# A two-layer hybrid step: weight slots of the head, the prompt's queries, and the order of the latent norm

## The reference, cut to what matters

```python
sh1, sc1, g1, sh2, sc2, g2 = split(silu(c) @ w_mod + b_mod, 6)     # modulation
h = rmsnorm(x, norm1) * (1 + sc1) + sh1
z = h @ w_in                                                        # 1024 x 2464
#   conv(768) | q latent 256, kv latent 128, rope 32 | retention q k v g 1024 | pooling 256
ckv = rmsnorm(z_kv, mla_kv_norm); q = rmsnorm(z_q, mla_q_norm) @ w_uq    # latent attention
x = x + g1 * (concat(y_conv, y_mla, y_ret, y_pool) @ w_out)
h = rmsnorm(x, norm2) * (1 + sc2) + sh2
q = h @ w_q                                     # PEER: 8 heads, 128 columns each
s = q . subkeys                                 # two halves x 128 keys a head
eidx, gates = top 16 of the 16 x 16 best pairs, softmax
a = h . u_tab[eidx]; y = sum_k gates * gelu(a) * v_tab[eidx]       # 128 rows of u and v a token
x = x + g2 * y
```

## Time and profile before

| | |
|---|---|
| median of three runs | 2587.06 us (2586.25 to 2589.85) |
| profiled execution | 2589.36 us, span 2587.6 us |
| TensorE matmul busy | 1896.0 us, 73% |
| VectorE busy | 1691.5 us, 65% |
| ScalarE busy | 550.9 us, 21% |
| GpSimd busy | 1518.4 us, 59% |
| moved | 939.90 MB, 363 GB/s over the span |
| mean granted TensorE clock | 0.89 of full |

### The profile page before, as it was taken

The page is one execution under the profiler, slowest core; times in us unless marked ns, Lnnn a source line. Parts: engine busy times, 40 slices in busy tenths (PEclk is TensorE's granted clock), DMA queues, the critical chain, the costliest instruction groups (busy, mean ns, idle before and its releaser), DMA issues.

```text
span 2587.6 us, 19654 instructions
## 1 busy us (share of the span) xinstructions
PE 1896.0 (73%) x5402; PEld 858.3 (33%) x5402; DVE 1691.5 (65%) x3756; ACT 550.9 (21%) x1378; POOL 1518.4 (59%) x1562
## 2 busy tenths in 40 slices
PE   5778985786777555697767677677777777777776
PEld 2354443353232212243342233334422322222222
DVE  0327875777799655566779666677868887554454
ACT  1332223221121101212222122222211121111111
POOL 2004554656677534656656655556667777677774
PEclk8988987898999866897889988788989999999999
DMA  8756996999999999999999999789999999999998
GB/s 291 259 193 248 405 354 238 385 364 399 385 403 409 403 396 371 356 355 405 337 404 383 361 375 383 288 291 385 358 375 409 409 409 409 371 411 409 409 409 323
DMA packets 295971, 939.90 MB, mean 363 GB/s; under 512 B 30692, under 2 KB 44360, under 8 KB 295864
## 3 DMA queue, kind: packets, MB, share of 16 engines
q0 software_dynamic: 222496, 809.28, 80.7%
q1 hardware_dynamic: 71304, 127.38, 13.6%
q10 hardware_dynamic: 2064, 2.00, 0.2%
HBM read 936.55 MB, written 2.00 MB: 363 GB/s over the span
## 4 chain that ended last, share of the span: by engine, by line
DMA 28%; DVE 25%; PE 24%; POOL 10%; issue 7%; ACT 5%; SPq 1%; DVEq 0%; ACTq 0%; POOLq 0%
DMA vbuf<-in_peer_v_dram,eidx 12%; DVE ubuf L2081 11%; DMA ubuf<-in_peer_u_dram,eidx 9%; PE ysum L1190 8%; PE bank L922 5%; POOL vbuf L2138 5%; POOL ubuf L2138 5%; DMA wring<-in_w_mod_dram 4%; DMA wring<-in_w_in_dram 3%; DVE acc L2074 3%; PE bank L1156 2%; PE bank L1141 2%; SPq L819 1%; PE bank L865 1%; DVE scratch L1955 1%
## 5 line engine op out<-in xcount | busy, mean ns | idle before, releaser
L1190 PE MATMUL ysum<-vbuf,diag 128*128 128x512 f32 x2356 | 1205.7, 647 | 356.4 <-DMA vbuf<-in_peer_v_dram,eidx 238.5
L2081 DVE CUSTOM_DVE_ANT_0 ubuf<-ubuf,h_bank 128x1024 f32<-128x1024 f32 x768 | 910.2, 1219 | 383.1 <-DMA ubuf<-in_peer_u_dram,eidx 356.2
L2138 POOL DMA_INDIRECT ubuf<-in_peer_u_dram,eidx x768 | 741.5, 966 | 620.0 <-DVE dot L2081 255.7
L2138 POOL DMA_INDIRECT vbuf<-in_peer_v_dram,eidx x768 | 763.5, 994 | 399.0 <-issue 184.9
L1190 PEld LDWEIGHTS ysum<-vbuf,diag 128*128 128x128 f32 x2356 | 440.7, 202 | 1074.9 <-DMA vbuf<-in_peer_v_dram,eidx 560.3
L1559 ACT ACTIVATE act_dot<-dot 128x4 f32<-128x4 f32 x192 | 39.4, 205 | 1252.9 <-DVE dot L2081 1251.4
L2074 DVE SCALAR_TENSOR_TENSOR acc<-vbuf,coef,acc 128x1024 f32<-128x1024 f32 x173 | 221.9, 1283 | 66.0 <-DMA vbuf<-in_peer_v_dram,eidx 55.2
L1570 ACT ACTIVATE diag<-ident,coef 128x128 f32<-128x128 f32 x589 | 201.0, 393 | 251.2 <-DVE coef L2086 201.4
L922 PE MATMUL bank<-wring,hT 128*128 128x512 f32 (+1 forms) x432 | 200.3, 621 | 30.4 <-DMA wring<-in_w_in_dram 24.0
L922 PEld LDWEIGHTS bank<-wring,hT 128*128 128x128 f32 x432 | 87.6, 205 | 137.9 <-issue 102.8
L865 PE MATMUL bank<-wring,cond 128*32 128x512 f32 x320 | 57.5, 854 | 62.5 <-DMA wring<-in_w_mod_dram 56.6
(11 more groups left out here) (267 smaller groups left out, 1285.3 us busy)
## 6 DMA issues: line engine op xcount, KB each, us to landing
wring<-in_w_mod_dram SPq DMA_DIRECT2D x24, 2048.0 KB, 18.6
wring<-in_w_in_dram SPq DMA_DIRECT2D x12, 2048.0 KB, 19.9
wring<-in_w_out_dram SPq DMA_DIRECT2D x8, 2048.0 KB, 19.3
wring<-in_peer_w_q_dram SPq DMA_DIRECT2D x8, 2048.0 KB, 18.7
ubuf<-in_peer_u_dram,eidx POOLq DMA_INDIRECT x768, 9.0
vbuf<-in_peer_v_dram,eidx POOLq DMA_INDIRECT x768, 9.1
wring<-in_w_in_dram SPq DMA_DIRECT2D x8, 1024.0 KB, 13.4
wring<-in_w_in_dram SPq DMA_DIRECT2D x4, 1664.0 KB, 11.4
```

The lines of the kernel that those rows point to most:

```text
L1190: mm = pe.matmul(ysum[:, b, :], diag[:, (n - 1) % DIAGS, :], vbuf[:, pick % V_SLOTS, 512 * b:512 * b + 512], start=first and r == rows[0], ...
L2081: dve.tensor_tensor_reduce(ubuf[:, n % U_SLOTS, :], ubuf[:, n % U_SLOTS, :], h2_bank[:, :, :].rearrange("p b n -> p (b n)"), 1.0, 0.0, ALU ...
L2138: pool.indirect_dma_start(buf[:, n % slots, :], None, rows, bass.IndirectOffsetOnAxis(eidx[:, t % 2, p:p + 1], 0))\
```

## The change

1. **Four slots in the head.** The first 19 blocks (up to the prompt's w_q) rotate over four slots: the two of `wring`, `ubuf[:, 0:4]` and `vbuf[:, 1:5]`. A block waits for the block that last held its slot. From block 19 on there are two slots as before.
2. **The prompt's queries with tokens held** (both layers). Two beats "qw": 8 products each with the tokens (hT) in the array and 512 columns of w_q moving, a ScalarE copy to `query_row`; two beats "qt": four transposes each into a bank, and a copy of four heads to `qpT`. The weights in `beats()` change from 8 x 1.7 to 5.2, 5.2, 1.7, 1.7.
3. **Order of the side beats.** `mla`'s first beat is now the first side beat, behind the turn of "conv"; the logarithms stand behind "mixed", the decay stage behind the turn of "mixed", then the two sums of squares behind "qk" and its turn, and the keys behind "rvg". The mixers begin with `ret`. ScalarE's wait for "rvg" in `mla` moves behind the norm.
4. **`kvn` has its own load and semaphore**: for layer 0 the first DMA that GpSimd issues, ahead of its wait for block 3.

```diff
@@ -155,6 +155,8 @@
     assert kind == "q"
+    if nt == 1:
+        return [(5.2, [("qw", m, b)]) for b in range(2)] + [(1.7, [("qt", m, b)]) for b in range(2)]
     return [(1.7 * nt, [("qp", m, h)]) for h in range(PEER_H)]
@@ -225,7 +227,8 @@
         for b in range(2):
-            yield ("peer_w_q", LAYER[a[0]], [(512 * b, 512)], ("qp", a[0], 4 * b + 3))
+            last = ("qw", a[0], b) if len(TILES[a[0]]) == 1 else ("qp", a[0], 4 * b + 3)
+            yield ("peer_w_q", LAYER[a[0]], [(512 * b, 512)], last)
@@ -410,12 +415,12 @@
     project_0 = [beat for _, beat in beats_of([("in", 0)])]
-    side = [beat for _, beat in beats_of([("logs",), ("rms", 1), ("rms", 2), ("keys", 0), ("decay", 0)])]
+    side = [(("mla", 0), 0)] + plain([("logs",), ("decay", 0), ("rms", 1), ("rms", 2), ("keys", 0)])
     order += project_0[:IN_FIRST]
...
         order += [beat] + side[len(side) * k // n:len(side) * (k + 1) // n]
-    order += side_by_side(mixers(0), mod_stages(0, range(4, 10)) + [("modscale", 0, 2)])
+    order += side_by_side(mixers(0)[1:], mod_stages(0, range(4, 10)) + [("modscale", 0, 2)])
     order += queries(0) + [(("score", 0), 0)] + rows_of(0)
@@ -507,15 +512,19 @@
     RING, TAKEN, USES, ORDER, BANK, BLOCKS, VALUE = plan()
-    WSLOTS = 2
+    WSLOTS, HEAD_SLOTS = 2, 4
     block_at = {}
...
-    landed_at, per_slot = [], [0] * WSLOTS
+    head_blocks = block_at["peer_w_q", 0, ("qw", 0, 1)] + 1
+    slot_of, held_by, landed_at, per_slot = [], [], [], [0] * HEAD_SLOTS
     for n, (_, _, cols, _) in enumerate(BLOCKS):
-        per_slot[n % WSLOTS] += 16 * len(cols)
-        landed_at.append(per_slot[n % WSLOTS])
+        at = n % HEAD_SLOTS if n < head_blocks else n % WSLOTS
+        held_by.append(max((k for k in range(n) if slot_of[k] == at), default=None))
+        slot_of.append(at)
+        per_slot[at] += 16 * len(cols)
+        landed_at.append(per_slot[at])
@@ -607,6 +616,8 @@
         product = pT[:, :, :].rearrange("p g n -> p (g n)")[:, 0:512]
+        query_row = [product, o_tok[:, :, :].rearrange("p i n -> p (i n)")]
@@ -742,6 +755,13 @@
+        def block_home(n):
+            if slot_of[n] < WSLOTS:
+                return wring[:, slot_of[n], :, :]
+            rows = ubuf[:, 0:4, :] if slot_of[n] == WSLOTS else vbuf[:, 1:5, :]
+            return rows.rearrange("p r (k n) -> p (r k) n", n=512)
         def span(tiles):
@@ -758,7 +778,7 @@
-            loads = [(rel[:, :, :], c["rel"]), (kvn[:, :], a["mla_kv_norm"][l].partition_broadcast(P)),
+            loads = [(rel[:, :, :], c["rel"]),
                      (w_uq[:, :, :], a["mla_w_uq"][l].rearrange("(k p) h d -> p k (h d)", p=P)),
@@ -798,14 +822,15 @@
                 what, layer, cc, last = BLOCKS[n]
-                if n >= WSLOTS:
-                    sp.wait_ge(bank_filled[slot(*BLOCKS[n - WSLOTS][3])], use(*BLOCKS[n - WSLOTS][3]))
+                if held_by[n] is not None:
+                    key = BLOCKS[held_by[n]][3]
+                    sp.wait_ge(bank_filled[slot(*key)], use(*key))
                 off = 0
                 for c0, w in cc:
-                    sp.dma_start(wring[:, n % WSLOTS, :, off:off + w],
+                    sp.dma_start(block_home(n)[:, :, off:off + w],
                                  a[what][layer].rearrange("(k p) n -> p k n", p=P)[:, :, c0:c0 + w])\
-                      .then_inc(w_landed[n % WSLOTS], 16)
+                      .then_inc(w_landed[slot_of[n]], 16)
                     off += w
@@ -1146,6 +1172,24 @@
                     pe.wait_ge(hT_ready, nth("hT", (2, t)))
+                if len(TILES[m]) == 1:
+                    for b in range(2):
+                        key = ("qw", m, b)
+                        w = weights("peer_w_q", LAYER[m], key)
+                        pe.wait_ge(bank_free[slot(*key)], use(*key))
+                        for k in range(DC):
+                            mm = pe.matmul(psum[slot(*key)][:, 0:512], hT[:, k, span(TILES[m])], w[:, k, :], start=(k == 0), stop=(k == DC - 1))
+                        mm.then_inc(bank_filled[slot(*key)], 1)
+                        yield
+                    for b in range(2):
+                        key = ("qt", m, b)
+                        pe.wait_ge(query_row_ready, nth("query_row", (m, b)))
+                        pe.wait_ge(bank_free[slot(*key)], use(*key))
+                        for i in range(4):
+                            mm = pe.transpose(psum[slot(*key)][:, P * i:P * i + P], query_row[b][:, P * i:P * i + P], ident[:, :])
+                        mm.then_inc(bank_filled[slot(*key)], 1)
+                        yield
+                    return
                 for b in range(2):
@@ -1372,10 +1416,10 @@
-                act.wait_ge(bank_filled[slot("rvg", TILES[m][-1])], use("rvg", TILES[m][-1]))
                 for t in TILES[m]:
...
                     yield
+                act.wait_ge(bank_filled[slot("rvg", TILES[m][-1])], use("rvg", TILES[m][-1]))
                 if s == 1:
@@ -1513,6 +1557,23 @@
                     act.wait_ge(state_stored, 16 * (LAYER[m] + 1))
+                if len(TILES[m]) == 1:
+                    for b in range(2):
+                        key = ("qw", m, b)
+                        act.wait_ge(bank_filled[slot(*key)], use(*key))
+                        act.activation(query_row[b], psum[slot(*key)][:, 0:512], ACT.Copy).then_inc(bank_free[slot(*key)], 1)
+                        act.wait_ge(bank_free[slot(*key)], use(*key) + 1)
+                        act.sem_inc(query_row_ready, 1)
+                        yield
+                    for b in range(2):
+                        key = ("qt", m, b)
+                        act.wait_ge(bank_filled[slot(*key)], use(*key))
+                        act.activation(qpT[:, 4 * b:4 * b + 4, span(TILES[m])], psum[slot(*key)][:, 0:512].rearrange("p (h n) -> p h n", h=4), ACT.Copy)\
+                           .then_inc(bank_free[slot(*key)], 1)
+                        act.wait_ge(bank_free[slot(*key)], use(*key) + 1)
+                        act.sem_inc(qp_ready, 4)
+                        yield
+                    return
                 for h in range(PEER_H):
@@ -1768,6 +1829,7 @@
                         dve.wait_ge(dve_done, steps[0])
+                    dve.wait_ge(kvn_landed[l], 16)
                     dve.scalar_tensor_tensor(out=lat[:, i, Q_LORA:Q_LORA + KV_LORA], in0=zc, scalar=stat[:, 19:20],
@@ -2151,7 +2213,8 @@
-            pool.wait_ge(w_landed[(FIRST_BLOCKS - 2) % WSLOTS], landed_at[FIRST_BLOCKS - 2])
+            pool.dma_start(kvn[:, :], kv_norm(0)).then_inc(kvn_landed[0], 16)
+            pool.wait_ge(w_landed[slot_of[FIRST_BLOCKS - 2]], landed_at[FIRST_BLOCKS - 2])
             for dst, src in SMALL:
...
```

More of the change, by code:

```diff
@@ L305, in announced @@
     elif kind == "q":
+        if len(TILES[a[0]]) == 1:
+            yield from (("query_row", (a[0], b)) for b in range(2))
         yield from (("qp", (a[0], h)) for h in range(PEER_H))
@@ L343, in queries @@
         got = woven("out out out out first out first second second", {"out": ("out", m), "first": ("ln", 2, ts[0]), "second": ("ln", 2, ts[1])})
-    return got + [(("q", m), i) for i in range(PEER_H)]
+    return got + [(("q", m), i) for i in range(len(beats(("q", m))))]
 def rows_of(m):
@@ L674, in hybrid_step @@
         qp_ready = sem("qp_ready")
+        query_row_ready = sem("query_row_ready")
         scores_ready = sem("scores_ready")
@@ L690, in hybrid_step @@
         layer_landed = [sem(f"layer_landed{l}") for l in range(DEPTH)]
+        kvn_landed = [sem(f"kvn_landed{l}") for l in range(DEPTH)]
         cache_stored = sem("cache_stored")
```

9 lines of the change are left out of this document (6 added, 3 removed).

## The result

The changed kernel takes 2579.49 us (median of 8 runs, 2576.18 to 2588.34); the kernel before took 2588.10 in the same comparison (8 runs, 2584.59 to 2595.35). The ratio is 0.9971 (95% interval 0.9960 to 0.9982): 7.5 us faster, between 4.7 and 10.4. The forecast was 17.

The account below looks back on a forecast made before the run. The head, ending at 232 us, was taken as where time could be won: 6.8 + 6.8 + 2.0 + 2.3 - 0.6 - 0.2 = 17.1; 2587.06 - 17 = 2570 us. Whole range 2563 to 2582; own range 2565 to 2576.

Parts of the forecast that it names:

- Part 4: End of the mixers: shorter weight waits at modulation rows 8 and 9 and an earlier square root; 2.3 us gained, bounds 1 and 3.
- parts 1: Projection up to "mixed": four weight slots, conv 8.5 us earlier, 2.5 of clock, -1.7 waiting for block 6; 9.3 us gained.
- 2: Projection from "mixed" to "rvg": earlier decays delay the "qk" copies, -2.6, and clock, -0.8; keys behind "rvg", +0.9 us.
- Reading what bounds the kernel: The head, ending at 232 us with the first dot product, is where time can be won; its gain arrives at the end.
- Part 3: Behind "rvg": latents' transposes no longer wait for DVE, 6.8 us gained, plus 2.0 (0 to 2.6) of clock.
- separate load of the norm's weights: Start of the head: the norm weights' own load delays the first block, costing 0.2 us.
- hold of the square root: End of the mixers: row 9's copy moves behind the square root, which can follow DVE's sums by 0.6 us; 1.3 us gained.
- Part 5: Prompt's queries with tokens held, up to the scores: 18.6 us instead of 18.0, a loss of 0.6, bounds 0 and 1.5.
- Block 5 lands no earlier: Rival in the projection: GpSimd's bytes take what the deeper queue was to win, conv starts at 56; 2580 us, 18%.
- The rows give it back: Rival in the row stages: near the transfer limit they lose the head's gain, 0 to 5 us remain; 2584 us, 8%.
- GpSimd's loads did not starve: Rival in the head: GpSimd's layer loads starve behind SP's full queue and hold up decays and projection; 2591 us, 4%.
- More than forecast: Rival in the head: block 6 early as well, clock up throughout; 22 to 26 us gained, 2563 us, 6%.

Follow-up runs that it names:

- late search: The changed kernel with eight unused DVE operations of 1.22 us ahead of tile 0's search, about 10 us; 2588.06 us, ratio 1.0006 to the kernel before.
- late_x: The changed kernel with GpSimd's sub-key and sample x loads held until block 6 has landed; 2578.43 us, ratio 0.9962 to the kernel before.
- decay_back: The changed kernel with the decay stage behind the last projection block again, latent norm still first; 2580.06 us, ratio 0.9976 to the kernel before.
- old_queries: The changed kernel with the prompt's queries as before (weights held, eight beats) in both layers; 2579.46 us, ratio 0.9971 to the kernel before.
- the combination: The changed kernel with logarithms and decays moved earlier (decays behind conv's turn), modulation rows at former places and old queries; 2572.98 us, ratio 0.9946.
- best_x: The combination with GpSimd's sub-key and sample x loads held until block 6 has landed; 2566.06 us, ratio 0.9918 to the kernel before.
- two_slots: The changed kernel with two weight slots in the head instead of four; 2587.47 us, ratio 1.0003 to the kernel before.
- mod_places: The changed kernel with modulation rows 4 to 9 at their former places among the mixers; 2578.07 us, ratio 0.9968 to the kernel before.

## Why the prediction was right in kind and wrong in size

The side was right, and the measured time lies in the range given, at its upper end and outside the forecast's own range (2565 to 2576). Two steps failed. Part 4, the end of the mixers, was forecast as a gain of 2.3 us and was a loss of 1.6. And parts 1 and 2 together were 3.0 us short, 2.2 of it at the "mixed" block, whose wait the forecast priced without the clock that TensorE loses by it. Step by step:

**Reading what bounds the kernel: right, with the wrong mark.** That the head is where time can be won, and that its gain is kept, held: from the first gather to the end all the kernels shown took 2363 to 2374 us, with no trend over heads that differ by 24 us. But I called the first dot product the head's end. The late search shows the gathers' start to be it. For this change both marks give the same number (10.7 us in the means of three), so the step cost nothing here.

**Part 1, four slots: right for conv, too high by 2.2 us behind it.** Conv started at 49.4, 47.4 and 48.1 and took 7.03, 8.83 and 7.03 (forecast 48 and 7). Where it had to wait for block 5, in four profiles of kernels with four slots, it started at 46.8 to 47.6, so the block landed about then (forecast 46). "mixed" was forecast for 58 and started between 58.4 and 59.0 in all ten profiles of kernels with four slots and GpSimd's loads not held back, whenever conv had finished (54 to 57 us). So the earlier conv is, the longer TensorE waits, and behind waits of 1.3 to 3.2 us the block took 8.5 to 10.2 us; behind the four waits of under 0.8 us it took 7.13. Holding back GpSimd's later loads (late_x) brought the block to 53.9 and "mixed" to 55.3 without a wait: what pinned it was that it shared the DMA engines with them. I had priced the wait (-1.7) and the clock that conv gets back (+2.5), but not the clock that the new wait takes away again: 1.1 us on average. The other 1.1 are the start itself (8.2 gained, not 9.3): block 6 landed 0.6 to 0.9 us later than forecast, and the mean of the kernel before is 67.0 and not 67.2.

**Part 2, decays earlier: right in mechanism, 0.8 us short.** The gap before the last projection block is 3.64 us (forecast 3.5), ended by ScalarE. From the start of "qk" to that of the last block it is 11.6 us, 9.4 before: 2.2 lost, where 2.6 - 0.9 was forecast. The block took 8.0 to 8.2 us, 1.1 over 7.03 where I took 0.8. By the estimate from the Trainium skill (ScalarE: Activation LUTs, What ACT_TABLE_LOAD costs) the three table loads in front of it would have made the gap 4.1 us longer; the measured 3.64 speaks for the load's own 1.28 us alone. That moving the decays gained next to nothing on balance is the result of decay_back; placed behind conv they bring the copy of "rvg" 4 us forward, of which the first gather kept 1.9.

**Part 3, latent norm first: right.** 9.8 us, where 6.8 + 2.0 was forecast: the stretch takes 7.7 us in each of the three profiles. The query product took 1.56 us instead of 2.83, as forecast. The 0.2 us for the separate load of the norm's weights I can't find. In the changed kernel this gain doesn't scatter; where the modulation rows or the decays stand elsewhere, 1.0 to 1.4 us of it were lost to a slower query product in four of five profiles, besides decay_back.

**Part 4, the end of the mixers: wrong in sign, the largest miss (3.9 us).** "Blocks 13 and 14 land by 98 and 104", and row 9's copy "behind that square root": the blocks landed at about 100 and 105, 12 us ahead of their rows, and the copy stands there, and it gave nothing. The two DMA waits (1.15 + 1.81 = 2.96) are gone. In their place stand, in the fence of the mixers' end, a row's sums that follow the row at once and wait for ScalarE's copy (0.49 and 0.87; another 0.87 at 114.91 had its equal before), DVE's product (0.58) and ScalarE (0.89): 2.83. The forecast had no such term. Taking one beat out of the weighting had moved all the modulation beats, not only row 9.

Then the hold of the square root: I had counted its table load as hidden, but in the new place it begins at 121.52, behind DVE's sums, so only 0.3 us of the 1.3 came (from the start of the sums' last operation to the square root 2.2 us in the earlier trace rows, 1.8 now: the load's end); row 9's copy (0.58) then stood in front of the next ones and took more than that. And the sums of the last row took 1.87 us and the last gate 1.92, where the first profile of the kernel before shows 1.05 and 1.16: behind the wait of 4.01 us that ends at 124.09 the granted clock is 0.50 up to the output projection. The other two profiles of the kernel before show 1.87 for the sums too. So between the first profiles 2.6 us are lost, between the means 1.6, since the kernel before scatters here (38.2 to 40.3 us) and the changed one doesn't (40.7 three times). Putting the beats back won 3.0 in this stretch.

**Part 5, queries: 1.3 lost, 0 to 1.5 forecast.** In the bounds, but the forecast's own pieces (15.7, 0.6, 0.65, 0.6, 1.5) add up to 19.05 us, not 18.6: a loss of 1.1 before any handover. From the first query matmul to the first score copy the three profiles show 19.2, where the earlier trace rows has 18.0. old_queries returned 0.7 of the 1.3 with no change in the time.

**The sum.** 17.1 less 3.0 (parts 1 and 2), plus 1.2 (part 3), less 3.9 (part 4) and 0.7 (part 5) is 10.7, the gain of the head. The three profiled executions of each kernel differ by 11.8 us in their mean time (2588.6 and 2576.8). The timed medians differ by 8.6 and the ratio gives 7.5: the changed kernel's three profiles lay 2.7 us below its own median. How much of the last 3 us is the draw of executions and how much a loss behind the head isn't settled. Over the kernels both signs occur: the combination showed 18.6 us in the head (mean of two) and 14 in time, the one with held loads 16.7 and 10, best_x 19.1 and 21.

**The rivals.** "Block 5 lands no earlier" fell with conv at 47.4 to 49.4; but its mechanism, GpSimd's bytes, struck one block later. "The rows give it back" isn't supported: a loss of up to 3 us can't be excluded (in two_slots 4 us of the head did not show in the time), not the 12 to 17 that it asked for. GpSimd's loads did not starve: the decays' last exponential ran at 74.58, and the tables were there. By the Trainium skill (DMA: Bandwidth & Descriptors, Queues, rings and completion order) the engines take turns between queues; the trace agrees as far as 54.9% and 49.9% of their time for the two queues from 36 to 56 us go, but it doesn't show the turns, and the 8.9% of SP's queue from 36 to 40 us in the earlier trace rows is no even share. "More than forecast" did not come: block 6 was not early.

## What to carry to other kernels

When a buffer is added so that a transfer starts earlier, price the next transfer behind it too, with the clock that TensorE loses while it waits for it: the gain ended here at the first block that still shared the engines with a bulk load, and holding that load back by some 14 us released it. Work that is moved in a chain handed from engine to engine should keep something between a producer and its consumer; a removed DMA wait is worth nothing if the round trip to ScalarE shows in its place. Measure a head by the start of the first transfer of the stage behind it, if that stage is bound by transfers, and take more than one profile of it: here the same kernel's first gather moved by 2 to 8 us from one execution to the next.

## What the runs showed of the hardware

**How much SP's queue takes.** With free slots one might expect the issues to follow at once. Timeline of SP, the changed kernel:

```profile
5.33 3.27 SPq L839 DMA_DIRECT2D x<-in_x_prompt_dram  x1
...
9.51 5.82 SPq L831 DMA_DIRECT2D vbuf<-in_w_mod_dram  x1
...
28.20 14.04 SPq L831 DMA_DIRECT2D ubuf<-in_w_in_dram  x2
42.28 9.64 SPq L831 DMA_DIRECT2D vbuf<-in_w_in_dram  x1
```

Block 5's issue took 0.37 us with two slots (row 34.42 of the earlier trace rows) and 5.29 with four; block 7's took 9.64, and of the two of block 6 in the row of 14.04 us the second took 11.5. At each of these times two or more earlier blocks had not landed whole (block 4 landed at 34.1, block 5 at 46.8). So I take it that the queue held the issue until older packets were through, and that slots beyond these would not bring transfers forward. Neither is shown: no run had any other number of slots than two or four.

**Short waits and the clock.** Blocks of the same 16 matmuls, which take 7.03 us behind no wait, took 7.13 us behind each of the four waits for weights of 0.5 to 0.8 us. Behind waits of 1.3 to 2.0 us they took 7.13 us three times and 8.8 twice, behind 2.1 to 3.2 us 8.5 to 10.2, behind 7.3 to 8.6 us 8.7 to 10.0. The wait alone doesn't settle it: 2.68 and 3.20 us cost less than 2.34 and 2.63. The first gather of one kernel varied by 2.3 us (changed), 2.6 (before) and 7.6 (combination) between executions.

**Where a table load stands.** At the end of the changed kernel's mixers, ahead of the square root, the table load of 1.28 us began only behind DVE's sums, after 3.37 us in which ScalarE was idle: there it cost its full length, though there was time to hide it. In mod_places it began at 123.92, before the sums were done (124.15), straight behind row 9's copy.
